# Compressed attention scores of a two-block transformer kernel: heads paired in one 128-row product, or each head alone in a 64-row product

## The reference

```python
s_c = jnp.einsum('bghsd,bgnd->bghsn', qh, kc).astype(jnp.float32) * scale   # 4 groups x 4 heads, d = 64, n = 15
s_c = jnp.where(valid_c, s_c, NEG_INF)
p_c = jax.nn.softmax(s_c, axis=-1) * jnp.any(valid_c, axis=-1)[:, None].astype(jnp.float32)
o_cmp = jnp.einsum('bghsn,bgnd->bghsd', p_c.astype(vc.dtype), vc)
```

## Time and profile before

| | before |
|---|---|
| median of 3 runs | 1270.22 us |
| the profiled execution | 1268.94 us, span 1267.1 us |
| PE busy | 1243.5 us (98%) |
| DVE, ACT, POOL busy | 820.9, 663.3, 194.1 us |
| granted TensorE clock | 0.999 of full speed |

### The profile page before, as it was taken

How to read it: one execution, slowest core, us unless ns; L and a number is a source line. 1 busy time by engine, 2 the same in 40 slices (tenths; PEclk the granted TensorE clock), 3 DMA queues, 4 the chain that set the end, 5 groups by cost and what they waited for, 6 DMA issues and landing times.

```text
span 1267.1 us, 16847 instructions
## 1 busy us (share of the span) xinstructions
PE 1243.5 (98%) x6398; PEld 1047.2 (83%) x6398; DVE 820.9 (65%) x979; ACT 663.3 (52%) x982; POOL 194.1 (15%) x162
## 2 busy tenths in 40 slices
PE   8999999999999999999999999999999999999998
PEld 6788888888887888888888898888997778888886
DVE  5898655455669866545547756875695687745544
ACT  5667464444555755443445455654546745543443
POOL 5884100000278720000000000000000030000000
PEclk9999999999999999999999999999999999999999
DMA  7523355556363253654555464342324445555551
GB/s 263 190 93 129 133 205 193 197 173 218 133 217 104 92 184 136 229 183 182 199 187 189 170 238 152 129 150 102 122 110 168 181 172 194 199 182 182 199 200 49
DMA packets 34219, 213.12 MB, mean 168 GB/s; under 512 B 4305, under 2 KB 5585, under 8 KB 11506
## 3 DMA queue, kind: packets, MB, share of 16 engines
q1 hardware_dynamic: 34098, 212.21, 47.0%
q0 software_dynamic: 64, 0.13, 0.0%
HBM read 211.28 MB, written 1.05 MB: 168 GB/s over the span
## 4 chain that ended last, share of the span: by engine, by line
PE 90%; DVE 6%; ACT 2%; issue 1%; POOL 0%; DVEq 0%; ACTq 0%; POOLq 0%
PE bank L587 25%; PE bank L589 25%; PE bank L588 25%; PE bank L1003 3%; PE bank L694 2%; PE bank L753 2%; DVE wlo L1711 1%; PE bank L713 1%; PE bank L842 1%; PE bank L615 1%; ACT probs L1321 1%; DVE z L2195 1%; PE bank L678 1%; PE bank L922 1%; DVE index L1829 1%
## 5 line engine op out<-in xcount | busy, mean ns | idle before, releaser
L1711 DVE TENSOR_TENSOR wlo<-raw,whi 128x2048 fp32r<-128x2048 f32 (+4 forms) x197 | 441.5, 2245 | 241.6 <-ACT whi L1244 240.3
L1244 ACT ACTIVATE whi<-raw 128x2048 fp32r<-128x2048 f32 (+5 forms) x201 | 369.3, 1842 | 132.9 <-PE bank L589 126.1
L587 PE MATMUL bank<-whi,hT_hi 128*128 128x512 f32 (+4 forms) x1040 | 406.4, 391 | 5.0 <-DVE wlo L1711 2.7
L589 PE MATMUL bank<-whi,hT_lo 128*128 128x512 f32 (+4 forms) x1040 | 397.5, 382 | 0.0
L588 PE MATMUL bank<-wlo,hT_hi 128*128 128x512 f32 (+4 forms) x1040 | 397.2, 382 | 0.0
L587 PEld LDWEIGHTS bank<-whi,hT_hi 128*128 128x128 f32 x1040 | 195.9, 188 | 44.4 <-issue 5.7
L589 PEld LDWEIGHTS bank<-whi,hT_lo 128*128 128x128 f32 x1040 | 195.8, 188 | 36.3
L588 PEld LDWEIGHTS bank<-wlo,hT_hi 128*128 128x128 f32 x1040 | 196.2, 189 | 33.0
L587 PE MATMUL bank<-whi,mixT_hi 128*128 128x512 f32 (+1 forms) x248 | 95.5, 385 | 3.3 <-issue 3.1
L587 PE MATMUL bank<-whi,ffT_hi 128*128 128x512 f32 x240 | 93.7, 390 | 0.0
L589 PE MATMUL bank<-whi,ffT_lo 128*128 128x512 f32 x240 | 93.5, 390 | 0.0
(11 more groups left out here) (283 smaller groups left out, 1462.0 us busy)
## 6 DMA issues: line engine op xcount, KB each, us to landing
raw<-in_ff_loop SPq DMA_DIRECT2D x90, 1024.0 KB, 4.8
raw<-in_w_groups SPq DMA_DIRECT2D x64, 1024.0 KB, 4.8
raw<-in_w_out SPq DMA_DIRECT2D x8, 1024.0 KB, 5.7
raw<-in_ff_first SPq DMA_DIRECT2D x6, 1024.0 KB, 4.7
raw<-in_w_values SPq DMA_DIRECT2D x8, 728.0 KB, 4.2
raw<-in_w_comp SPq DMA_DIRECT2D x4, 1024.0 KB, 6.7
raw<-in_ff_last SPq DMA_DIRECT2D x3, 1024.0 KB, 7.1
raw<-in_w_values SPq DMA_DIRECT2D x4, 736.0 KB, 6.6
```

Source lines behind the costliest of these rows:

```text
L587: eng.matmul(out, lhsT=hi, rhs=wh, start=start, stop=False)
L589: return eng.matmul(out, lhsT=lo, rhs=wh, start=False, stop=stop)
L1244: eng.activation(whi[j][:, 0:n], raw[j][:, 0:n], ACT.Copy).then_inc(hi_ready, 1)
L1711: eng.tensor_tensor(wlo[j][:, 0:n], raw[j][:, 0:n], whi[j][:, 0:n].bitcast(F32), ALU.subtract).then_inc(lo_ready, 1)
```

## The change

The scores are formed with one head for each matmul. The keys are copied once, as they are (128 x 60, one ACT instruction in place of two); they stand on both halves of the partitions already, since line 1095 writes them twice. A matmul takes 64 rows (one head's half of `headsT`) and 15 columns. All even heads of both r go to bank 2, then all odd heads to bank 3: 2 x 16 = 32 matmuls in place of 16. They all come after `product_chunk(9, 0)`, none between its halves. DVE adds the mask in four pieces of 8 x 15 in place of two of 16 x 15. POOL's blank area shrinks by the 256 columns of the keys.

```diff
-            eng.memset(headsT[:, T2_KC:T2_V + 4, :], 0.0).then_inc(blank_ready, 1)
+            eng.memset(headsT[:, T2_V:T2_V + 4, :], 0.0).then_inc(blank_ready, 1)
...
-            def compressed_scores(r):
-
-                eng.wait_ge(read67[0], 7)
-                for i in range(8):
-                    g = i // 2
-                    mm = eng.matmul(bank[2 + r][:, i * 32:(i + 1) * 32], lhsT=headsT[:, i, r * P:(r + 1) * P],
-                                    rhs=headsT[:, T2_KC, g * 32:(g + 1) * 32], start=True, stop=True)
+            product_chunk(9, 0)
+
+            eng.wait_ge(read67[0], 7)
+            for odd in range(2):
+                half = slice(HD * odd, HD * odd + HD)
+                for r in range(RT):
+                    for i in range(8):
+                        g = i // 2
+                        mm = eng.matmul(bank[2 + odd][:, r * P + i * 16:r * P + i * 16 + CMP],
+                                        lhsT=headsT[half, i, r * P:(r + 1) * P],
+                                        rhs=headsT[half, T2_KC, g * CMP:(g + 1) * CMP], start=True, stop=True)
                 mm.then_inc(cs_ready, 1)
-
-            product_chunk(9, 0, between=lambda: compressed_scores(0))
-            compressed_scores(1)
             product_chunk(9, 1)
...
-            eng.wait_ge(blank_ready, 1)
-            for odd in range(2):
-                half = slice(HD * odd, HD * odd + HD)
-                ins = eng.activation(headsT[half, T2_KC, 0:4 * 32].rearrange("p (g o n) -> p g o n", o=2, n=16)[:, :, odd, 0:CMP],
-                                     bank[6][half, 0:COMP // 2].rearrange("p (g n) -> p g n", n=CMP), ACT.Copy)
-                if odd:
-                    ins.then_inc(read67[0], 1)
-                else:
-                    act(ins)
+            eng.activation(headsT[:, T2_KC, 0:COMP // 2], bank[6][:, 0:COMP // 2], ACT.Copy).then_inc(read67[0], 1)
...
-            for r in range(RT):
-                eng.wait_ge(cs_ready, r + 1)
-                dve(eng.tensor_tensor(probs[:, r, :].rearrange("p (h n) -> p h n", n=32)[:, :, 0:CMP],
-                                      bank[2 + r][:, 0:SEQ].rearrange("p (h n) -> p h n", n=16)[:, :, 0:CMP],
-                                      cmask[:, r, :].unsqueeze(1).to_broadcast([P, 16, CMP]), ALU.add))
+            for odd in range(2):
+                eng.wait_ge(cs_ready, odd + 1)
+                for r in range(RT):
+                    dve(eng.tensor_tensor(probs[:, r, :].rearrange("p (h o n) -> p h o n", o=2, n=32)[:, :, odd, 0:CMP],
+                                          bank[2 + odd][:, r * P:(r + 1) * P].rearrange("p (h n) -> p h n", n=16)[:, :, 0:CMP],
+                                          cmask[:, r, :].unsqueeze(1).to_broadcast([P, 8, CMP]), ALU.add))
```

## The result

The changed kernel takes 1277.11 us (median, 1276.97 to 1277.48); the kernel before takes 1270.22 on the same chip. The ratio is 1.0051, 95% interval 1.004 to 1.0063: slower by 5 to 8 us, where 2.2 had been forecast and the range ended at 1275.2. The profiled execution took 1276.94 us, span 1275.0.

What follows compares the result with a forecast made beforehand. PE was taken as busy throughout, with the chain from last score through DVE to product 10 setting the end. The last score's +2.05 and the adds' +0.18 gave 2.2 us: 1270.22 + 2.2 = 1272.4 us, range 1270.0 to 1275.2.

Steps and rivals of the forecast that it cites:

- The bounding chain: From the last score through DVE and ACT to DVE's low part, then product 10: forecast 2.2 us later.
- its own test: The argument would be wrong if product 10 moved by another amount than DVE's last add.
- A pass costs 0.112 us at 64 rows and 15 columns: PE's new score block: each pass taken at 0.1116 us, bounds 0.056 to 0.112.
- its rivals: For the new score block: serial 1274.2 us (chance 0.18), full overlap 1270.6 (0.15), faster 1269.8 or 1268.9 (0.07).
- Going in and out costs 0.39 us: PE's score block: entering and leaving 64-row work costs 0.39 us once; the 128-row scores had none.
- The halves overlap by 16 passes: PE's score block: 16 odd-head passes run beside even ones, so 64 passes last as long as 48; block 5.75 us.
- DVE's adds, +0.18 us: DVE's mask adds behind the last score: two for the odd heads take 0.60 us against 0.43 before.
- The place, the single copy on ACT, the smaller memset cost nothing: Moving scores behind the chunk, ACT's one copy and POOL's smaller clear were claimed to add no time.
- PE keeps its waits of 0.9 and 1.1 us: PE's waits ahead of the transposes and of product 10 were to stay at 0.9 and 1.1 us.
- serial: PE's score block: odd passes wait for all even ones, block 7.53 us, kernel +4.0 us, 1274.2 us; chance 0.18.

Runs made afterwards that it cites:

- the alternating block: Changed kernel with each even head's matmul followed by the odd one's, behind product chunk (9, 0): 1271.44 us against 1270.61, ratio 1.0006.
- the split kernel: Changed kernel with the even heads' 16 matmuls in the middle of product chunk (9, 0), the odd heads' behind it: 1277.71 us against 1270.61, ratio 1.0051.

## Why the prediction was wrong

The bounding chain was read rightly: product 10 starts when DVE's low part is done, DVE starts when the last score lands, and what arises here is not given back later. Product 10 moved by 7.87 us and DVE's last pair of adds by 7.82, which is what the prediction asked for as its own test. Two terms of the sum before that chain failed: the length of the overlap, and the clock, which the sum does not have. Step by step:

- *A pass costs 0.112 us at 64 rows and 15 columns*: right as long as the clock is up (the first 2 us of the block, and the alternating block), wrong from then on. The prediction does not speak of the clock: it takes every price from rows at full clock (the page's clock row is all nines) and carries it over to the changed kernel. But the clock depends on what PE does, as the run with 128 columns shows, and the change alters just that: fewer columns for each pass, twice as many passes, all in one block. The block lasted from 766.65 to about 777.9, 11.2 us; at full clock its 60 slots would have been 7.1. This term, absent from the prediction and from its rivals, is 4.1 us in the profiled execution (3.97 between the traces with 15 and 128 columns, product 9 to 10), and 2.8 us between the medians of the two.
- *Going in and out costs 0.39 us*: borne out in the main: 7.20 us less the 61 passes counted by their starts leaves 0.39, and 3.87 us (767.65 to 771.53, alternating) less 32 leaves 0.30.
- *The halves overlap by 16 passes*: wrong, three or four. The 17 weight loads between the sequencer's wait and its matmul show how far the queue reaches along one kind of work. The start of the other half's passes reaches only some four passes, as the runs with 1, 4 and 16 matmuls in a row show. Rows 5, with its runs of just four passes, could not tell these apart, and rows 7 count passes on one kind of work: the depth of the queue was taken for the reach of the overlap. The term is mis-sized by 12 slots, 1.3 us.
- *DVE's adds, +0.18 us*: 0.07, in a single execution of the kernel before.
- *The place, the single copy on ACT, the smaller memset cost nothing*: borne out for the place (ratio 0.9996). The other two were not tried alone; the sum below leaves about 0.05 us for them.
- *PE keeps its waits of 0.9 and 1.1 us*: right at full clock (0.81 and 1.11 with 128 columns), wrong in the change, where the slow chunk ate them up.

The sum: DVE's first add for the odd heads moved by 777.84 - 770.02 - 0.32 = 7.5 us, where 2.05 was forecast; 1.3 from the overlap and 4.1 from the clock make up the 5.45. In medians, each against the kernel before beside it, it is 3.7 us with 128 columns and 6.9 for the change. That the medians show about 1 us less than the two profiled executions is not settled. The kernel before has executions with a lower mean clock (0.995 to 1.0, 1269.3 to 1274.9 us), which raise its median above its profiled execution; none of them was profiled. Eight of the other traces have one more fall of 3.4 us far from the scores, three near 125 us and five near 454 us, and neither the kernel before nor the change has one in its trace.

The rival "serial" was near in its mechanism (4.0 us against 3.7 at full clock; its 64 passes one by one were 60 or 61), and even it did not reach the result.

## What to carry to other kernels

Splitting a block-diagonal matmul into two on halves of the rows doubled the passes here, and a pass took 0.112 us at 15, 32 and 128 columns alike. So nothing was saved: with the halves alternating in program order the block took 3.87 us against 3.57, and one half after the other 7.20. Before small matmuls are gathered in one block, or thinned out, ask what the clock will do: the page's clock row tells of the kernel as it is. Where a chain through another engine sets the next start, moving its source ahead of independent PE work can pay: moved by half a chunk, the old scores brought product 10 1.95 us nearer, more than any other form of the scores that was run.

## What was not expected of the hardware

- PE was busy all the time, and still the granted clock fell in the traces of the change, of 128 rows with 15 columns and of 128 rows with 32 in an equally long block, and not in the block with 128 columns. The other executions have only a time and a mean clock. They fit a fall in all twelve of the change (1275.9 to 1277.7 us, mean 0.994 to 0.996), in all four with 128 rows and 15 columns (1275.3 to 1277.4, 0.994 to 0.996), in three of six with 32 columns, and in none of nine with 128 (1273.6 to 1275.9, 0.997 to 1.0).
- Whether a single block of about 4 us with 15 columns lowers it differs: in the profiled executions it did where it stood in the middle of the chunk, split or alternating, and behind the chunk in groups of four matmuls, but not behind the chunk alternating one by one. What decides that is open.
- It can fall behind the small matmuls: 0.8 us after the block of the split kernel, during matmuls of 358 columns.
- Streaming 128 columns where 15 are needed made the kernel 2.8 us faster (medians; 3.3 by the ratios).
- TensorE: Matmul & The Clock Gate, The mechanism (the Trainium skill), has matmuls start in program order and the window 64 deep. These traces differ from both: 64 passes in the time of 61 can't come from strict order, and with a reach of 64 they would have taken that of 32. The odd heads' passes ran beside the last three or four even ones, and not beside those further ahead of them.
